# Two unused margins in SBUF move the weight ring and the activation buffers to multiples of 1024 bytes

## The reference, cut to what matters

```python
# first block, two layers: mLSTM + stick-breaking mixer, or gated DeltaNet mixer
x = x + ab_mixer(rmsnorm(x, g), w_in, ..., w_out)       # 1024 x 3072, 1024 x 1024; layer 1: 1024 x 4096
x = x + mem_cross_attn(rmsnorm(x, g), memn, wq, wk, wv, wo)   # four 1024 x 1024
x = x + jnp.square(jax.nn.relu(h @ w1)) @ w2            # 1024 x 4096, 4096 x 1024
...
# second block, two layers: two sparse/gated attentions, or block attention
h = x @ w_up                                            # 1024 x 5632
g = conv_general_dilated(h[..., :2816], conv_w) + conv_b
x = x + (jax.nn.silu(g) * h[..., 2816:]) @ w_down       # 2816 x 1024
```

## The kernel before

| tensors | start before | modulo 1024 |
|---|---|---|
| `ring_hi`; `ring` and `ring_lo` | 16,512; 41,088 | 128 |
| `consts`, `smalls` | 65,664; 84,384 | 128; 416 |
| `xT`, `x_hi`, `x_lo`, `memn`, `sq`, `mix_hi`, `mix_lo`, `work` | 91,328 and on | 192 |
| `rstd`, `cosT`, `sinT`, `stream_f` | 217,504 and on | 416 |

## Time and profile before

### The profile page before, as it was taken

How to read it: one execution, slowest core, us unless ns; L and a number is a source line. 1 busy time by engine, 2 the same in 40 slices (tenths; PEclk the granted TensorE clock), 3 DMA queues, 4 the chain that set the end, 5 groups by cost and what they waited for, 6 DMA issues and landing times. The chain is left out here.

```text
span 1659.3 us, 32586 instructions
## 1 busy us (share of the span) xinstructions
PE 1583.7 (95%) x12614; PEld 1508.7 (91%) x12614; DVE 765.7 (46%) x1392; ACT 833.1 (50%) x1252; POOL 1190.6 (72%) x920
## 2 busy tenths in 40 slices
PE   7989999999999899999999999989999998999997
PEld 6878989999998788998999998869999997899997
DVE  6647244220076656544422005955554228465521
ACT  4664455554465544555555445455545444555442
POOL 5654976988967600496699896806999997189995
PEclk9998999999999989999999999989999999899999
DMA  7332534555544300353455554305556553155552
GB/s 284 128 102 96 184 127 153 185 186 189 187 157 152 115 1 1 103 178 128 153 190 185 185 191 140 127 26 166 192 194 197 193 192 115 52 178 187 185 188 102
DMA packets 67662, 248.56 MB, mean 150 GB/s; under 512 B 7632, under 2 KB 7888, under 8 KB 67152
## 3 DMA queue, kind: packets, MB, share of 16 engines
q1 hardware_dynamic: 67536, 246.71, 44.8%
HBM read 245.63 MB, written 1.05 MB: 149 GB/s over the span
## 5 line engine op out<-in xcount | busy, mean ns | idle before, releaser
L343 POOL TENSOR_TENSOR ring_lo<-ring,ring_hi 128x512 fp32r<-128x512 f32 x916 | 1190.4, 1335 | 449.3 <-ACT ring_hi L987 446.9
L987 ACT ACTIVATE ring_hi<-ring 128x1024 fp32r<-128x1024 f32 x458 | 465.9, 1051 | 203.9 <-DMA ring<-panels 195.9
L377 PE MATMUL ps_dve<-x_hi,ring_hi 128*128 128x256 f32 x1928 | 468.5, 281 | 15.7 <-POOL ring_lo L343 10.9
L377 PE MATMUL ps_dve<-x_lo,ring_hi 128*128 128x256 f32 x1928 | 464.1, 279 | 0.0
L377 PEld LDWEIGHTS ps_dve<-x_hi,ring_hi 128*128 128x128 f32 x1928 | 362.2, 188 | 21.9 <-issue 15.0
L377 PEld LDWEIGHTS ps_dve<-x_lo,ring_hi 128*128 128x128 f32 x1928 | 362.3, 188 | 0.5 <-issue 0.2
L377 PE MATMUL ps_dve<-x_hi,ring_lo 128*128 128x256 f32 x1928 | 275.6, 279 | 0.0
L377 PEld LDWEIGHTS ps_dve<-x_hi,ring_lo 128*128 128x128 f32 x1928 | 247.2, 188 | 0.8 <-POOL ring_lo L343 0.6
L377 PE MATMUL ps_dve<-work_parts,ring_hi 128*128 128x256 f32 x1728 | 231.7, 279 | 0.0
L377 PEld LDWEIGHTS ps_dve<-work_parts,ring_hi 128*128 128x128 f32 x1728 | 217.1, 188 | 0.0
L1472 DVE TENSOR_TENSOR xT<-xT,ps_dve 128x512 f32<-128x512 f32 x40 | 27.5, 688 | 336.6 <-PE ps_dve L377 336.6
(11 more groups left out here) (272 smaller groups left out, 2023.5 us busy)
## 6 DMA issues: line engine op xcount, KB each, us to landing
ring<-panels SPq DMA_DIRECT2D x458, 512.0 KB, 3.3
consts<-constants SPq DMA_DIRECT2D x1, 2208.0 KB, 12.7
xT<-x_t SPq DMA_DIRECT2D x1, 1024.0 KB, 5.0
memn<-mem_t SPq DMA_DIRECT2D x1, 1024.0 KB, 19.1
out_t<-xT SPq DMA_DIRECT2D x4, 256.0 KB, 2.3
smalls<-small_operands SPq DMA_DIRECT2D x1, 824.5 KB, 15.7
consts<-constants SPq DMA_DIRECT2D x1, 129.5 KB, 4.9
angle_i<-positions SPq DMA_DIRECT2D x1, 128.0 KB, 7.9
```

The costliest lines, as they stand in the source:

```text
L343: pool.tensor_tensor(ring_lo[:, s, cs], ring[:, s, cs], plain(ring_hi[:, s, cs]), ALU.subtract).then_inc(sem("lo_made"), 1)
L377: ins = pe.matmul(o, lhsT, rhs, start=start, stop=stop, skip_group_check=True)
L987: tell(act.activation(ring_hi[:, n % RING, :], ring[:, n % RING, :], ACT.Copy), "hi_made")
```

## The change

Two tensors that nothing reads or writes are allocated: `ring_margin` of 224 float32 (896 bytes) ahead of `ring_hi`, and `stream_margin` of 240 float32 (960 bytes) ahead of `xT`. No instruction is added, removed or moved on any engine; only addresses change.

```diff
+        sb("ring_margin", [P, 224])
         ring_hi = sb("ring_hi", [P, RING, PANEL * P], F32R)
         ring, ring_lo = sb_over("ring", "ring_lo", [P, RING, PANEL * P], F32, F32R)
         consts = sb("consts", [P, N_CONST])
         smalls = sb("smalls", [P, N_SMALL])
+        sb("stream_margin", [P, 240])
         xT = sb("xT", [P, C, T])
```

## The result

The changed kernel is slower. Its median is 1689.32 us (1684.66 to 1696.42, four executions), that of the kernel before 1669.97 us (1667.11 to 1673.94, four); the ratio is 1.0118, 95% interval 1.0072 to 1.0164. The forecast was 1671 us, no change, within 1650 to 1681. The profiled execution has a span of 1682.9 us, against 1659.3.

The account below looks back on a forecast made before the run. PE's ring matmuls, start to start, were taken as the bound, plus parts where PE waits for DVE and ACT. All terms were 0: 1661.0 + 0 = 1661.0 us for the profiled execution, median about 1671 us, range 1650 to 1681.

Parts of the forecast that it names:

- What bounds the kernel: PE's 10,992 ring matmuls start to start, at 118 or 113.4 ns, plus parts where PE waits for DVE and ACT.
- Step (1): PE's ring steps under the new operand starts: between 39.5 us less and 12.0 us more, taken as 0.
- (2): ACT's and POOL's passes over the ring, 1051 and 1298 ns: they lie beside PE, taken as 0.
- (4): DMA writes into the ring: only the first panel isn't hidden, 0.3 us bounds it, taken as 0.
- Step (3): DVE's and ACT's own work on the path, 149 us: 0.9% bounds it at 1.3 us either way, taken as 0.
- Step (5): Pace lottery at halts: small timing changes can flip the pace, 7.0 us per ffn stage, 7.2 us per MLP stage.
- Rival B: Every ring step: equal low bits collide, 1673 to 1677 us or 1723; chance 0.16 together with another rival.
- Rival A: Ring steps: equal low bits help, all or many go to 113.4 ns, 1620 us, about 1646 with half; chance 0.19.

Follow-up runs that it names:

- e1: Only `ring_margin` of 224 float32 added to the kernel before, distance 64 in `project`: median 1669.17 us of ten, ratio 1.0016.
- f3: `ring_margin` of 224 and `stream_margin` of 288 float32 added to the kernel before, distance 192 in `project`: 1643.41 us, one execution.
- g1: The layout of f3 once more, timed against the kernel before: median 1646.96 us of six executions, ratio 0.9878.

## Why the prediction was wrong

**What bounds the kernel** was right, and so was the measure: the loss is in PE's start-to-start pace, 36 us of it, less 12 us that came back in the parts between. That a pace of 118 or 113.4 is set at a halt and then kept is nearly borne out. In the four profiled executions at 64 and 192 (before, e1, f3, g1) there are ten changes without a halt (no distance above 124 ns), three of them in the trace before, and all ten stand where `project` hands over to `project_tokens` or back, that is where the distance changes from one of the two to the other. In nine of the ten the distance goes from 64 to 192 and the pace from slow to fast; in one (g1, at 58 us) it goes from fast to slow. I hadn't seen the three in the trace before; they already say that the distance has a part in it. At 0 there is nothing to switch.

**Step (1) failed**, in two places. First, "between these I take 0, because the same addresses show both paces in full": that one layout allows two paces says nothing of what another layout does. The distance of the two streams was 64 in every ring step of `project`, and 192 in tokens, so the trace held no row for 0. I said so and still let the argument from the halts decide. The token rows were a hint that I didn't take: at the opposite distance they were fast in 55% of the steps, against 24% in `project`. Second, the bound was wrong: I took 118.0 as the worst pace, 12.0 us above the profiled execution. Distance 0 has its own pace of 119.8 to 120, 1.8 ns more than the slow pace of the earlier trace rows and 6.4 more than the fast one.

The rows on starts 12 bytes or 4 bytes off prove less than I took from them, since they are durations and not paces. A load lasts 188 ns in the trace before whether the step takes 113 or 118 ns, and at distance 96, where the mean step takes 120.0, it lasts 188.3; so 189 against 188 for `ones` can't show that a start costs nothing. The matmuls of 65 and of 128 columns follow each other at the same 112 ns (the median of each group), so something other than the columns read sets their pace. And no row of them has the two streams of a 256-column fp32r step at another distance.

The count of fast steps was low: the trace before has 2,832 steps of 113 or 114 ns, not 2,554. Two of the windows behind that sum, x197 in 24.00 us and x121 in 15.00, average 122 and 124 ns because they hold other matmuls, and the first some halts. That moves the 12.0 us to 13.3 and changes nothing in the argument.

**Steps (2) and (4)** stand: POOL 1299 against 1298 ns, ACT 1051, and PE waits for L345 for 11.0 us once at the start and 2.4 us in all after that (before: 10.9 and 3.2), its weight loads for 4.0 us (before: 4.8); it waits for `ring_hi`, and so for a DMA at most, for 1.4 us (before: 2.4). Step (3) is not tested: DVE's busy time fell by 9.7 us, 1.3%, more than the 0.9% that the step allowed, and over all layouts it lies between 747 and 766 us without following the distance.

**Step (5)**, the lottery, is real inside an execution: f3 and g1 are one kernel and have 71% and 85% fast steps. It wasn't what moved the median, and that it makes the scatter between executions is not shown. At distance 0, where there is one pace, four executions still lie between 1684.66 and 1696.42 us. At 192 the fastest (1637.14 us) had a mean clock of 0.983 and the slowest (1654.76) one of 0.972, which by the estimate above is 18 us, all of their difference. So reading the three timed runs as executions with less of the fast pace was unproven too.

**Rival B** was the right mechanism, with its place and its cause: load and moving operand now start alike, and collide. Its first form, fast stretches vanish, happened, and its price was too small (1673 to 1677 us) because it too was bounded by 118; its second, a further quantum of 4.68 ns on each step, was too large. The real step was 3.3 ns on the mean of 10,838. Its point of decision, 0.46 ns a step, was passed seven times over. I gave it a part of 0.16, because the pace turned at a halt with addresses unchanged and because of a rule. The Trainium skill, "SBUF — State Buffer", section "Who interferes with whom", has PE's two read ports independent and PE waiting on no one. The run with `work_parts` at 0 contradicts it for fp32r steps of 128 x 128 by 256: 120.0 ns against 115.5 in one execution, by the distance of the two reads. The load of 188 ns, which the prediction took as agreeing with the rule, is the same at both paces and can't bear on it. The other figure of the Trainium skill, 109.2 ns ("TensorE: Matmul & The Clock Gate", section "Back-to-back issue gap"), is given there for an isolated matmul, which the prediction left out; the lowest pace of a long stretch in any run is 113.0 (g1).

**Rival A** was wrong for distance 0 and right in part for 192, where 71% to 85% of the steps in `project` are fast and the rest still slow.

What stays open: what inside the chip makes the two streams meet in a pattern of 256 bytes, why 113.4 and 118 both exist at 64 and 192, and what about a halt picks one of them. The runs give the pace by distance; none looks inside.

## What to carry to other kernels

Where TensorE is the bound, read its pace per step from a long stretch without idle time, and compare it over stages: two paces for the same shape at the same clock are a difference of unknown cause on every step, and here it was worth more than any wait. Before buffers are padded, compute the distance between stationary and moving operand modulo 256, not the alignment of each; for this shape, of the nine distances tried, 0 and 96 are the worst and 192 is the best, and it costs one or two unused tensors to try. A row bounds only the relation that it shows, so where a change makes a relation that no row has, give the mechanism that would use it a price beyond the rows and a larger chance.

## What the runs showed of the hardware that wasn't expected

- A float32r step (128 x 128 loaded, 256 columns moving) takes a mean of 114.0 to 120.0 ns start to start at the same granted clock of 2.4 GHz, by the distance of its two operands in SBUF. Of the nine distances tried in `project`, 192 has the lowest mean and 0 and 96 the highest. With POOL, ACT and DVE all idle the pace at 0 is 119.9 all the same.
- It is the distance and not the place: ring and activations both at 128 modulo 1024 cost the same (ratio 1.0114) as both at 0 (1.0118).
- The order of the two streams matters: 96 gives 120.0 and 160 gives 118.3, 32 gives 116.9 and 224 gives 118.3, whichever buffer is the moving one.
- At 64 and 192 two paces exist, 113 to 114 and 117 to 119 ns; an execution changes between them at halts, and ten times in four executions where the two operands swap roles. One layout had 71% fast steps in one execution and 85% in another.
- The duration of a weight load doesn't tell the pace: it is 188 ns in steps of 113 and of 118 ns, 188.3 at a mean of 120.0 (distance 96) and 192 at distance 0.
